# A hybrid attention and mLSTM trunk on one core: scores of two heads in turn, blocks in falling length, and another order in the first FFN steps

## The reference

```python
h = modulate(rms_normalize(x), sh1, sc1)
x = x + 0.5 * gt1 * swiglu(h, w_ffn1_in, w_ffn1_out)
h = modulate(rms_normalize(x), sh2, sc2)
y = hybrid_mixer(h, ...)          # forgetting attention, 8 heads x 64, beside mLSTM, 4 heads x 128
x = x + gt2 * y
h = modulate(rms_normalize(x), sh3, sc3)
x = x + 0.5 * gt3 * swiglu(h, w_ffn2_in, w_ffn2_out)
return rms_normalize(x) * g_final

# forgetting attention, a block of 128 queries:
logits = einsum('qd,kd->qk', q_i, k) * scale + c_i[:, None] - cum[None, :]
logits = where(pos_i[:, None] >= kpos[None, :], logits, -inf)
p = softmax(logits)
return einsum('qk,kd->qd', p, v)
```

## Time and profile before

| | us |
|---|---|
| median of 3 runs | 2113.92 |
| the profiled execution, as timed | 2113.61 |
| its span, from the first to the last instruction | 2111.9 |
| TensorE busy in the span | 1965.1 (93%) |
| VectorE, ScalarE, GpSimd busy | 1171.6, 758.1, 886.3 |
| mean granted TensorE clock | 0.966 |

### The profile page before, as it was taken

One profiled execution on the slowest core, in us unless ns is written; L12 is line 12 of the kernel. 1 busy time (PEld: TensorE's weight loads), 2 busy tenths in 40 slices (PEclk: granted clock), 3 DMA queues, 4 the chain that ended last, 5 costly groups with the idle time before them and its releaser, 6 DMA issues. The chain is left out here.

```text
span 2111.9 us, 25584 instructions
## 1 busy us (share of the span) xinstructions
PE 1965.1 (93%) x9248; PEld 1621.5 (77%) x9248; DVE 1171.6 (55%) x1748; ACT 758.1 (36%) x1363; POOL 886.3 (42%) x636
## 2 busy tenths in 40 slices
PE   4599999999999979999998999798799999999997
PEld 3478888888888757888887777686688888888886
DVE  5857666655777741443322466537544453457777
ACT  4523232222444431443321444425233233324444
POOL 4867677674000341000002111358787887830002
PEclk8799999999999979999999999899999999999999
DMA  7245665633965111100101110132232322249662
GB/s 291 66 136 178 197 193 177 208 111 121 386 215 191 51 30 51 41 16 25 60 11 50 41 40 20 60 130 85 77 122 100 115 100 85 80 146 378 204 192 88
DMA packets 204613, 257.10 MB, mean 122 GB/s; under 512 B 14014, under 2 KB 124882, under 8 KB 202962
## 3 DMA queue, kind: packets, MB, share of 16 engines
q1 hardware_dynamic: 204498, 255.59, 36.2%
HBM read 206.71 MB, written 48.84 MB: 121 GB/s over the span
## 5 line engine op out<-in xcount | busy, mean ns | idle before, releaser
L420 POOL TENSOR_TENSOR ffn_ring_b<-ffn_raw_in,ffn_ring_b 128x512 fp32r<-128x512 f32 x172 | 242.5, 1416 | 159.1 <-ACT ffn_ring_b L415 159.1
L832 PE MATMUL bank<-ffn_w_hi,ffn_a_hi 128*128 128x512 f32 x616 | 240.2, 390 | 1.2 <-DVE ffn_w_lo L816 1.2
L834 PE MATMUL bank<-ffn_w_hi,ffn_a_lo 128*128 128x512 f32 x616 | 239.7, 389 | 0.0
L833 PE MATMUL bank<-ffn_w_lo,ffn_a_hi 128*128 128x512 f32 x616 | 239.6, 389 | 0.0
L1525 POOL TENSOR_TENSOR mx_w_lo<-mx_raw_w,mx_w_hi 128x1024 fp32r<-128x1024 f32 x29 | 72.9, 2522 | 389.7 <-ACT mx_w_hi L1355 389.6
L415 ACT CAST ffn_ring_b<-ffn_raw_in 128x512 fp32r<-128x512 f32 x172 | 106.4, 620 | 291.3 <-PE bank L1259 276.4
L108 POOL TENSOR_SCALAR rms<-rms 128x1 f32<-128x1 f32 x24 | 15.1, 628 | 444.3 <-ACT ffn_junk L102 430.6
L1257 PE MATMUL bank<-h_hi,ffn_ring_a_hi 128*128 128x512 f32 x360 | 144.9, 402 | 44.6 <-issue 17.5
L1083 DVE TENSOR_TENSOR ffn_u<-bank,ffn_u 128x512 f32<-128x512 f32 x112 | 77.1, 688 | 170.3 <-PE bank L1259 170.3
L805 ACT CAST ffn_a_hi<-ffn_a_stage 128x512 fp32r<-128x512 f32 x154 | 95.6, 621 | 200.8 <-PE bank L834 196.0
L816 DVE TENSOR_TENSOR ffn_a_lo<-ffn_a_stage,ffn_a_hi 128x512 fp32r<-128x512 f32 x154 | 106.3, 690 | 73.9 <-ACT ffn_a_hi L805 73.8
(11 more groups left out here) (316 smaller groups left out, 4820.3 us busy)
## 6 DMA issues: line engine op xcount, KB each, us to landing
ffn_raw_in<-in_w_ffn_in SPq DMA_DIRECT2D x88, 512.0 KB, 5.9
ffn_a_stage<-hidden SPq DMA_DIRECT2D x154, 256.0 KB, 3.2
ffn_w_stage<-in_w_ffn_out SPq DMA_DIRECT2D x132, 256.0 KB, 2.9
ada_rest<-in_w_ada SPq DMA_DIRECT2D x64, 448.0 KB, 4.0
hidden<-ffn_u SPq DMA_DIRECT2D x88, 256.0 KB, 2.0
hidden<-ffn_g SPq DMA_DIRECT2D x66, 256.0 KB, 2.0
mx_raw_w<-in_w_mix_in SPq DMA_DIRECT2D x28, 512.0 KB, 3.8
ada_ring<-in_w_ada SPq DMA_DIRECT2D x8, 1024.0 KB, 12.1
```

What stands on the lines that cost most here:

```text
L420: pool.tensor_tensor(self.lo(q), self.source(b, m), self.hi(q).bitcast(F32), ALU.subtract)\
L832: pe.matmul(dst, a_hi, w_hi, start=first, stop=False, skip_group_check=True)
L833: pe.matmul(dst, a_hi, w_lo, start=False, stop=False, skip_group_check=True)
L834: mm = pe.matmul(dst, a_lo, w_hi, start=False, stop=True, skip_group_check=True)
```

## The change

It has three parts. **Attention:** items go in pairs (both heads of one block), with blocks 7, 6, ..., 0. `scores(p, q)` issues both heads' matmuls in turn, head 0 to banks 0 and 1, head 1 to banks 2 and 3, then both masks. The four projections for the next pair are no longer in two groups of two at the end: `STEP_OF` puts q of the second token half after q=5, k of the second half after q=6, q of the first half after q=7, and k of the first half in the middle of q=8; they go to banks 1 and 3, which short blocks leave free. **First FFN:** its first step takes the order `LATER`, so p3 with b22 comes sixth. **Both FFNs:** VectorE cuts the low parts of t1 and t4 in pieces of two between `make_u2` and `make_u3`.

```diff
-    def cut_lo(self, eng, op, after=None):
-        for k in range(4):
+    def cut_lo(self, eng, op, after=None, ks=range(4)):
+        for k in ks:
...
     def order(self, b):
-        return self.LATER if b else self.FIRST
+        return self.LATER if b else self.first
...
+    def p3_early(b):
+        return b == 0 and weights.first == InWeights.FIRST
...
             for b in range(STEPS):
                 hidden11(b)
-                if b == 0:
-                    halved.cut_lo(dve, "t1", after="t2")
-                    halved.cut_lo(dve, "t4")
...
                 make_u2(b, 0)
+                if b == 0:
+                    halved.cut_lo(dve, "t1", after="t2", ks=(0, 1))
                 make_u2(b, 1)
+                if b == 0:
+                    halved.cut_lo(dve, "t1", after="t2", ks=(2, 3))
...
                 make_u3(b, 0)
+                if b == 0:
+                    halved.cut_lo(dve, "t4", ks=(0, 1))
                 make_u3(b, 1)
+                if b == 0:
+                    halved.cut_lo(dve, "t4", ks=(2, 3))
...
-                if p == "p3" and b:
+                if p == "p3" and not p3_early(b):
                     pe.wait_ge(c22_made, 2 * b + 1 + g)
...
-    UP = [(n // 2 + NS // 2 - 1) % NS for n in range(PER)]
-    BLOCK = [(UP[n], NS - 1 - UP[n])[n % 2] for n in range(PER)]
+    BLOCK = [NS - 1 - n // 2 for n in range(PER)]
+    STEP_OF = {5: 1, 6: 3, 7: 0, 8: 2}
+    QK_ORDER = tuple(STEP_OF.values())
+    def qk_bank(p, g):
+        return core.bank[:, g if isinstance(p, int) and p == 0 else (1, 1, 3, 3)[g], :]
... TensorE
-            def scores(p, n, first):
+            def scores(p, q, first):
+                i = BLOCK[2 * q]
+                w, rows = (i + 1) * P, slice(i * P, (i + 1) * P)
+                heads = [slice(e * HD, (e + 1) * HD) for e in range(2)]
+                if q == 0:
                     pe.wait_ge(fq_cut, p * 4 + 4)
...
+                if not (first and q == 0):
+                    pe.wait_ge(logit_done, p * PER + 2 * q)
...
+                    for m, (left, right) in enumerate(((fq_hi, fk_hi), (fq_hi, fk_lo), (fq_lo, fk_hi))):
+                        for e in range(2):
+                            pe.matmul(core.bank[:, 2 * e + b, 0:k2 - k0], left[heads[e], rows], right[heads[e], k0:k2],
+                                      start=(m == 0), stop=(m == 2 and k1 < w))
+                for e in range(2):
+                    pe.matmul(core.bank[:, 2 * e + b, k1 - k0 - P:k1 - k0], ident_b[:, :], mask_f[:, :],
+                              start=False, stop=True).then_inc(score_ready, 1)
...
             def fox_body(p, first, last):
+                for q in range(1, NS + 1):
+                    if q < NS:
+                        scores(p, q, first)
+                    turn_prob(p, 2 * q - 2, first)
+                    if q > 1:
+                        values(p, 2 * q - 3, first)
+                    if q == NS and not last:
+                        pe.wait_ge(fq_cut, p * 4 + 6)
+                        project_qk(p + 1, STEP_OF[q])
+                    turn_prob(p, 2 * q - 1, first)
+                    values(p, 2 * q - 2, first)
+                    if q < NS and q in STEP_OF and not last:
...
+                        project_qk(p + 1, STEP_OF[q])
                 values(p, PER - 1, first)
                 if not last:
                     scores(p + 1, 0, False)
... VectorE
+                for q in range(1, NS + 1):
+                    if not last and q - 1 in STEP_OF:
+                        cut_qk(p + 1, STEP_OF[q - 1])
+                    if q < NS:
+                        logits(p, 2 * q, first)
+                    keep_pt(p, 2 * q - 2, first)
+                    if q < NS:
+                        logits(p, 2 * q + 1, first)
+                    elif not last:
+                        cut_qk(p + 1, STEP_OF[q])
+                    keep_pt(p, 2 * q - 1, first)
+                    if q > 1:
+                        normalise(p, 2 * q - 3, first)
+                    normalise(p, 2 * q - 2, first)
... last lines
-        ffn1_weights = InWeights(core, "f1", buf, w_ffn1_in)
-        ffn2_weights = InWeights(core, "f2", buf, w_ffn2_in)
+        ffn1_weights = InWeights(core, "f1", buf, w_ffn1_in, InWeights.LATER)
+        ffn2_weights = InWeights(core, "f2", buf, w_ffn2_in, InWeights.FIRST)
```

91 lines of the change are left out of this document (32 added, 59 removed).

## The result

The changed kernel takes 2078.14 us (median of 4 runs, 2075.65 to 2080.47) against 2114.49 for the kernel before in the same series: a ratio of 0.9829, interval 0.9812 to 0.9846. The forecast was 2089 with a range of 2079 to 2108. The direction was right; the time lies 11 us under the forecast and 0.9 under the range. The profiled execution took 2075.65, with a span of 2073.9, 38.0 less than before. In a later series the same kernel had a median of 2075.38. In that series both kernels also had executions that took 29 to 43 us more (one of 2118.34 after the change, five of 2143 to 2147 before it), and without them the times are 2075.12 to 2076.27 and 2113.76 to 2115.05.

The account below looks back on a forecast made before the run. TensorE, busy 93% of the span, was taken as the bound. FFNs 13.4 us, less 1.0, plus attention 12.0 (26.4 shed, 17.6 new waits, 3.2 old waits gone) gave 24.4 off 2113.61: 2089 us, range 2079 to 2108.

Parts of the forecast that it names:

- the floor under a couple of matmuls: Attention scores: each of 72 matmuls a pair still loads its weights, 0.114 us each, so 8.2 us remain of 13.2.
- a wait of 3.3 us ahead of p3: First FFN's first step: TensorE waits 3.3 us for c22(0), which VectorE delivers at 108.5, before p3.
- (a): Attention scores: going from 128-row to 64-row matmuls and back costs 0.2 us a group; 8 fewer groups save 1.6 a pair.
- (b): Attention scores: alternating heads use different array rows and overlap down to the weight loads, 5.0 us won a pair.
- rival 2: Attention scores: full overlap, weight loads too; a couple costs one matmul, 6.6 us a pair; 2082 us, chance 0.13.
- rivals 1 and 3: Attention scores: heads do not overlap, 2109 us, chance 0.14; or each change of rows drains, 2140 us, chance 0.05.
- New waits in the attention: Attention: TensorE waits at pair boundaries 2.7, logits 7.6, bank 5 copies 4.6, last pair 1.5, small ones 1.2; 17.6 us.
- FFN2: Second FFN's first step: second step's p2 starts 8.6 us earlier after a new 4.5 us wait; 7.6 after low clock.
- FFN1: First FFN's first step: reordered products and split low parts let the second step's p2 start 5.8 us earlier.
- rival 4: FFNs: waits are replaced as p4 or p3 waits for VectorE; 12.4 falls to about 5; 2096 us, chance 0.08.
- the 1 us for the low clock: Second FFN: after the new wait, eight or so matmuls run at 1.2 GHz, twice the price; 1 us taken off.
- a clock below 1 in the attention: Attention: the prediction named the clock falling below 1 there as a sign that it was wrong.

## Why the prediction was right or wrong

The path was right. Three terms failed: the floor under a couple of matmuls (6.4 us), the price of a change of rows (3.2), and the first FFN (4.5), where the effect of the order on the start was put at nothing and a wait of 3.3 us ahead of p3 didn't come. The lower end of the range, 2079, was full overlap with 16 us from the FFNs; with the start they gave 17.5, and no rival had more than 0.2 us a group for going between 128 and 64 rows.

- **Which resource.** Right: in the attention TensorE's work came off the time, and no wait appeared in the middle of a pair.
- **(a) Changes of rows**, 0.2 us a group: found, but undersized, 0.30 measured. I read it off the first and the last distance within a group; the 0.09 ahead of a group's first matmul was left out, hidden in the mean of the values that I took from rows 4. Over 32 groups fewer that is 3.2 us.
- **(b) Overlap.** Mechanism right, size wrong. The floor of 0.114 per matmul was taken from transposes and values, which all use the whole array. For two halves of the array it doesn't hold: a couple costs one matmul, 6.6 us a pair instead of 5.0, 6.4 in all. The overlap of rival 2 was true, and rivals 1 and 3 were not: the heads' products start in couples, at the price of one. With these two prices the forecast of 26.4 would have been 36.0; TensorE shed 33.6. Of the 2.4 between them 1.6 are the third pair's first scores at half the clock (58.33 us busy against 56.77), and 0.8 stay open. The Trainium skill had said it (TensorEngine Tiling (Array Packing), Key Properties: different tiles load weights and multiply in parallel), and the couples of after agree, 0.12 us for two matmuls of 256 columns. I gave it 0.13, since no row showed a load every 0.06 us; but no row showed two halves of the array either, so the nearest rows were no bound for them.
- **New waits in the attention**, 17.6 forecast: 16.57 of idle time measured. The logits' waits were right (2.65 forecast, 2.58; 1.65 forecast, 1.67), the copies' nearly (1.15, 0.95), and the last pair's and the small ones, 2.7 forecast, were 0.9. That at the boundary was 1.60 instead of 0.9, and another wait: a normalisation behind a low part in VectorE's queue. I had asked what is late for the scores, not what else is queued behind the operation that is late.
- **FFN2.** Right: 7.2 against 7.6, with the wait at p2 where and as long as forecast. p2 came 8.8 us earlier instead of 8.6, and the low clock behind it cost 1.6 instead of 1 (eight matmuls at 0.43 instead of 0.23).
- **FFN1.** 10.3 with its start, 9.7 to the end of the first product, against 5.8. The step that failed is "GpSimd, which is moved past nothing here": the order also sets what ScalarE's fifth and sixth casts wait for, ahead of the modulation. It is worth 3.5 us at the first product and 1.4 at p2. And the 3.3 us at p3 didn't come: VectorE's eight low parts took 10.9 us instead of 12.97, since GpSimd, waiting for later casts, left it alone in part. So rival 4 did not come either.
- **The sum.** 5.8 + 7.6 + 12.0 is 25.4, not 24.4: the 1 us for the low clock was taken off twice. By its own terms the forecast was 2088.
- **The clock.** The 38 us are no accident of it: in the second series after had 2075.1 to 2076.3 in five of six executions, and its first pair was 61.05 us again. But the sign of being wrong that the prediction named, a clock below 1 in the attention, did come: 0.97 in the third pair, 62.02 us instead of 60.98, and 0.97 in the second pair of the second profile, 62.07. It cost 1 us each time.

So of the 12.6 us between 25.4 and 38.0, 8.2 are the attention and 4.5 the first FFN with its start; FFN2 has 0.4 the other way.

## What to carry to other kernels

Products that use 64 of the 128 rows should stand beside products on the other 64: a couple costs one, down to 256 columns, as long as no full-height product stands between them; here TensorE found a partner that stood up to four places on by itself. Changes between full and half height cost 0.30 us out and back, so keep the half-height products of a block together. When a step is moved, follow every queue that holds something of it, and at a predicted wait look at what is queued behind the late operation. An operation of VectorE that is brought forward beside GpSimd wins little (0.5 of 4.4 us); one that is taken off VectorE wins more (3.2 of 3.9 us at the next product).

## What the runs showed of the hardware

- TensorE started a product ahead of three earlier ones of the program, when it used the other half of the rows (912.36 against 912.58).
- Two products on the two halves of the rows, with weights of their own, take as long as one: 0.23 us with 512 columns, 0.12 with 256. A change between 128-row and 64-row products and back takes 0.30 us.
- VectorE's operation on two SBUF inputs of 512 columns: 0.62 us alone, 1.7 beside GpSimd's.
- The clock in the attention: 1.00 in the first two pairs of after and 0.97 in the third, but 0.50 for over 62 us of the first pair with each head's mask between, where TensorE does more single 64-row products and was busy for 11.10 of 12.50 us ahead of the fall. Of kernels that wait the same at the boundary, some keep the clock and some don't, and single executions of one kernel differ. What tips it stays open.
